# Differential attention: the transposes of a query block ahead of the scores of the block two further on

## The reference

```
s = jnp.einsum('bqhmd,bkhmd->bhmqk', qb, keys).astype(f32) * ATTN_SCALE   # m = 0, 1
p = jax.nn.softmax(s, axis=-1)
a = p[:, :, 0] - lam * p[:, :, 1]
return jnp.einsum('bhqk,bkhe->bqhe', a.astype(vals.dtype), vals)
```

## Time and profile before

| what | us |
|---|---|
| median of three runs | 1901.68 |
| the profiled execution | 1904.32 |
| its span on the core | 1902.5 |
| PE busy, whole span | 1621.9 |
| DVE, ACT, POOL busy | 960.7, 743.9, 473.3 |
| first scores of head 0 | 1013.35 |
| first scores of head 7 | 1405.62 |

### The profile page before, as it was taken

The page is one execution under the profiler, slowest core; times in us unless marked ns, Lnnn a source line. Parts: engine busy times, 40 slices in busy tenths (PEclk is TensorE's granted clock), DMA queues, the critical chain, the costliest instruction groups (busy, mean ns, idle before and its releaser), DMA issues.

```text
span 1902.5 us, 23127 instructions
## 1 busy us (share of the span) xinstructions
PE 1621.9 (85%) x7996; PEld 1223.5 (64%) x7996; DVE 960.7 (50%) x2220; ACT 743.9 (39%) x1364; POOL 473.3 (25%) x193
## 2 busy tenths in 40 slices
PE   5299899979829999999569999999976969988877
PEld 3298666657617888888347777767755848754445
DVE  5011554437366867768764454555453265145633
ACT  4022555642343232323344444355443242246642
POOL 2144211114303445445212112111110323310002
PEclk9579999989959999999779999999997969979998
DMA  8833111116213545555301111011100212210001
GB/s 161 179 100 100 56 60 57 62 39 249 100 66 122 174 158 165 177 165 175 99 23 45 45 34 45 33 33 44 33 34 11 66 46 89 67 45 1 1 2 65
DMA packets 47728, 153.49 MB, mean 81 GB/s; under 512 B 5510, under 2 KB 7814, under 8 KB 47272
## 3 DMA queue, kind: packets, MB, share of 16 engines
q1 hardware_dynamic: 37000, 117.36, 20.2%
q10 hardware_dynamic: 10656, 35.20, 5.6%
HBM read 141.01 MB, written 11.53 MB: 80 GB/s over the span
## 4 chain that ended last, share of the span: by engine, by line
PE 75%; DVE 12%; issue 7%; ACT 4%; POOL 1%; DVEq 0%; DMA 0%; ACTq 0%; POOLq 0%; SPq 0%
PE ps L277 39%; PE ps L281 19%; PE ps L442 3%; PE ps L461 3%; PE ps L472 3%; PE ps L977 3%; PE ps L1013 2%; DVE b_sb L560 1%; DVE sqsum L323 1%; DVE xn L1543 1%; DVE x2l L1535 1%; PE ps L989 1%; DVE ropea L1562 1%; DVE tg L1437 1%; PE ps L327 1%
## 5 line engine op out<-in xcount | busy, mean ns | idle before, releaser
L804 POOL TENSOR_TENSOR w_l<-raw,w_h 128x1024 fp32r<-128x1024 f32 x189 | 473.1, 2503 | 1407.2 <-ACT w_h L264 1407.2
L264 ACT ACTIVATE w_h<-raw 128x1024 fp32r<-128x1024 f32 x189 | 200.0, 1058 | 588.6 <-PE ps L277 549.9
L277 PE MATMUL ps<-x2h,w_h 128*128 128x512 f32 x832 | 249.1, 368 | 46.8 <-DVE x2l L1535 21.3
L277 PE MATMUL ps<-x1h,w_h 128*128 128x512 f32 x584 | 240.5, 412 | 30.4 <-DVEq L1474 18.5
L277 PE MATMUL ps<-x2h,w_l 128*128 128x512 f32 x832 | 235.5, 352 | 0.0
L281 PE MATMUL ps<-x2l,w_h 128*128 128x512 f32 x832 | 234.6, 351 | 0.0
L281 PE MATMUL ps<-x1l,w_h 128*128 128x512 f32 x584 | 232.6, 398 | 0.0
L277 PE MATMUL ps<-x1h,w_l 128*128 128x512 f32 x584 | 232.5, 398 | 0.0
L277 PEld LDWEIGHTS ps<-x2h,w_h 128*128 128x128 f32 x832 | 134.9, 192 | 93.8 <-issue 48.2
L1504 DVE CUSTOM_DVE_ANT_0 terms<-mraw,crow 128x1024 f32<-128x1024 f32 x96 | 166.9, 1739 | 2.1
L277 PEld LDWEIGHTS ps<-x1h,w_h 128*128 128x128 f32 x584 | 113.2, 194 | 59.1 <-DVEq L1474 20.1
(11 more groups left out here) (235 smaller groups left out, 2440.7 us busy)
## 6 DMA issues: line engine op xcount, KB each, us to landing
raw<-in_w_mlp SPq DMA_DIRECT2D x64, 512.0 KB, 3.5
mraw<-in_w_mod ACTq DMA_DIRECT2D x51, 512.0 KB, 4.0
raw<-in_w_a SPq DMA_DIRECT2D x32, 512.0 KB, 3.5
raw<-in_w_att SPq DMA_DIRECT2D x25, 512.0 KB, 3.5
raw<-in_w_b SPq DMA_DIRECT2D x20, 512.0 KB, 3.5
raw<-in_w_g SPq DMA_DIRECT2D x16, 512.0 KB, 3.5
dbias<-brow SPq DMA_DIRECT2D x1, 5120.0 KB, 53.0
gates<-g_stage ACTq DMA_DIRECT2D x16, 256.0 KB, 2.0
```

The costliest lines, as they stand in the source:

```text
L264: nc.scalar.activation(w_h[:, u % SPL], raw[:, u % RAW], ACT.Copy).then_inc(w_hi, 1)
L277: mm = nc.tensor.matmul(o, w[:, u % SPL, k], xh(k), start=(first and k == k0 and wi == 0), stop=(last and k == k1 - 1 and wi == 1))
L804: nc.gpsimd.tensor_tensor(w_l[:, u % SPL], raw[:, u % RAW], w_h[:, u % SPL].bitcast(F32), ALU.subtract).then_inc(w_lo, 1)
```

## The change

In each of the four turns of the loop over query blocks the order on PE was scores(qt + 2), dense(2), turns(qt), dense(1 + qt % 2). It becomes dense(1 + qt % 2), turns(qt), scores(qt + 2), dense(2). So the transposes of block qt are issued ahead of the scores of block qt + 2, and the last pieces of one turn and the first of the next run without a break. No instruction is added or removed, and the other engines' lists are as they were.

```
                 scores(1)
                 dense(4)
                 for qt in range(4):
+                    dense(1 + qt % 2)
+                    turns(qt)
                     scores(qt + 2)
                     dense(2)
-                    turns(qt)
-                    dense(1 + qt % 2)
                 turns(4)
                 dense(2)
```

## The result

The changed kernel takes 1954.15 us in the median of four runs (1953.33 to 1956.69), the kernel before 1903.37 (1900.6 to 1905.85). The ratio is 1.0269, with a 95% interval from 1.025 to 1.0289: slower by 50.8 us, where 45.8 were forecast (1947.5, range 1930 to 1962). The profiled execution took 1954.16 us, 49.8 more than that of before.

The account below looks back on a forecast made before the run. PE's own list was taken to bound the seven heads; 29 us for their waits, 6.8 for clock falls and 10 for the eighth head made 45.8 on 1904.3, or 1950, less 2.6: 1947.5 us, range 1930 to 1962.

Parts of the forecast that it names:

- The order gives PE nothing: Switches between kinds of matmul on PE: within 0.1 us a turn, at most 5 us either way over 28 turns.
- the walk: Step-by-step timeline of PE over one of the seven heads: the head 4.15 us longer, seven heads 29 us.
- Rival 5: Faster: transposes ahead of scores cost no switch and merged pieces save both old ones, 6 us: 1896; chance 0.03.
- The waits for the copies: PE's first piece after the q and k units waits uncovered for ACT's copy, 1.06 us each.
- 0.25 at block 1, 0.75 at block 2: PE waits 0.25 us at turns(1) for turned(0), and 0.75 us at turns(2) for combine(2), in each of seven heads.
- The large term at block 4: turns(4) waits 2.7 us for combine(4) in place of 0.9, in each of seven heads.
- The rotation is shorter: DVE's rotation of q, ahead of combine(4), takes 2.75 us instead of 4.15, free of POOL's subtraction.
- The first rival: DVE's rotation of q keeps its 4.15 us, adding 10 us: 1957; chance 0.10.
- The clock in the seven heads: The wait ahead of turns(4) lowers PE's clock in four of seven heads at 1.7 us each: 6.8 us, bounds 0 to 11.9.
- the second rival: The clock stays at full speed in all seven heads and the eighth costs 6.7 us: 1937; chance 0.16.
- The eighth head: Without pieces the waits show in full: 6.7 us more at full clock, 10 with low clock, bounds 6.7 and 16.
- Rivals 3 to 5: 3: some waits shorter than walked, near 1930, 0.09; 4: waits only move idle time, 1902, 0.04; 5: faster, 1896, 0.03.

Follow-up runs that it names:

- the run of pieces alone: Kernel before the change, each turn's pieces put in one run between scores and transposes, transposes still behind scores: 1911.35 us, ratio 1.0044.
- dealt pieces: Changed kernel, with the pieces redistributed so that projection units end ahead of transposes and scores or the weighing: 1933.4 us, ratio 1.0139.
- the late rotations: Next head's q and k rotations moved behind combine(4) and combine(5): changed kernel 1930.32 us, kernel before 1899.12 us, the latter with pieces dealt too 1883.48 us.
- the cover put back: Changed kernel, with the two pieces behind the transposes of block 4 moved ahead of them: 1933.57 us, ratio 1.0162.
- The spare matmuls: Changed kernel, with 20 matmuls of unused result ahead of the transposes of block 4 in seven heads: 1946.84 us, ratio 1.0234.
- the spare matmuls in the eighth head: Changed kernel, with 30, 30 and 12 matmuls of unused result ahead of the eighth head's transposes of blocks 1, 2 and 3: 1951.55 us, ratio 1.0241.

## Why the prediction was right

- **Which stage, which engine.** Right: PE's own list bounds the seven heads, and its new waits are the loss.
- **The order gives PE nothing.** Right within its bounds. The starts of the walk are met to 0.2 us over a whole head, and the run of pieces alone gained nothing. (Rival 5 counts 32 turns where the eighth head has no pieces; 28 would give 5 us. It decides nothing.)
- **The waits for the copies** (1.06 each, 0.49 and 0.43 before), **0.25 at block 1, 0.75 at block 2.** Shown: as idle times 0.90, 0.99 and 0.61 (less by the modelled tails of the matmuls before), and at block 1 the start is right to 0.1. The experiment with dealt pieces took them away together, and met another wait of ACT's list that the walk had no reason to have. The signs also named about 1 us at v's unit; it is 0.8 there, the same as before the change, and no term of the sum.
- **The large term at block 4.** Right in size (1164.7 for 1164.6) and in cause: the late rotations and the cover put back each took it away.
- **The rotation is shorter, 2.75 for 4.15.** Right, 2.72. The first rival, worth 10 us, falls: the rotation moved clear of the subtraction in all seven heads. In two further kernels the clash came back on the two-input operation of DVE that began inside the subtraction: L1558 at 2.79 us and a 128 x 1 product at 1.76. That such an operation lasts until the POOL instruction ends is what the rows show. That a shared port is the cause comes from the Trainium skill ("SBUF — State Buffer", section "SBUF: two separate sides"); no run here tests it apart.
- **The clock in the seven heads.** Four falls at 1.7 forecast, five at 1.5 measured: 7.5 for 6.8. The spare matmuls show the cause; the second rival falls. The number was a guess between none and seven and its nearness is luck: with the same seven heads, the clock fell in six of them in the profiled execution of one kernel and in four in another.
- **The eighth head.** The term that was too small: 10 forecast, 13.0 measured. The rings at full clock were priced at 6.7 and come to about 7.6; the low clock was given 3.3 and took about 5.4 (both by the estimate above), since the transposes of blocks 1 to 4 and, but for part of the first, all four scores ran slow and lay on the path. The measured 13.0 is within the stated 6.7 to 16.
- **Rivals 3 to 5** needed `combine(4)` early or hand-overs shorter than their distance. PE waited 2.49 us for `combine(4)`, and idled 0.90 and 0.99 us at the copies, so they fall.

The forecast fell 6.7 us short of the median. From one profiled execution to the other the time grew by 49.8 us where the sum had 45.8. Of these 4.0 us, 1.0 comes from the heads' walk (30.0 for 29), 0.7 from the falls and 3.0 from the eighth head, less 0.7 in which the executions differ elsewhere. The other 2.6 are no term of the sum: I took them off because the profiled execution of before lay above its median, and that of the changed kernel does not.

## What to carry to other kernels

When work is moved on the bounding engine, write down for each semaphore it waits on the distance between the instruction that starts the other engines' path and the instruction that needs its end, in that engine's own time, before and after. The move here shortened the last such distance from 6.0 us (against a path of 6.9) to 2.8 (against 5.5). Follow every engine's list in the ring, not the busiest alone: three of the four misses of the experiments came from a list that was left out, ACT's copies twice and POOL's subtraction once (the fourth, the spare matmuls in the eighth head, came mostly from a clock that was already low). And deal filler (independent work such as the pieces) so that a hand-over of a shared buffer ends ahead of other work: here that was worth 16 us on top of the late rotations.

## What the runs showed of the hardware

- An idle time of 2.49 us on PE between dense matmuls was followed by the lower clock in five of seven heads, and not in the other two. With dealt pieces a wait of 2.47 us was mostly not followed by it, while one of 1.94 us was in one head, so the length of the wait alone does not decide. Filling the gap with spare matmuls was faster by 6 to 7 us than leaving it idle.
- DVE operations with two SBUF inputs that started inside a POOL subtraction lasted until it had ended, the small ones too: 128 x 1 values took 1.76 us in place of 0.16.
- Six transposes ahead of scores cost 0.75 us of PE and ahead of pieces 0.57, so moving them beside the scores neither gains nor loses much: the 0.18 us more is set against two switches of about 0.09 that the merged pieces no longer make.
